# Thirty-two recurrent rounds of an RWKV-7 and attention kernel: loop written out, group norm's end one round later, front steps in another order

## The reference

```python
def rwkv7_layer(h, ...):                       # layer A
    proj = token_shift(rmsnorm(h, norm) @ w_in, mu)   # u + mu * (prev - u)
    r, k, v, z = ...                           # 1024 columns each
    w_lo, a_lo = ...                           # 64 columns each
    w_log = -softplus(-(decay_bias + tanh(w_lo) @ decay_up)) - 0.5
    decay = exp(-exp(w_log))
    a = sigmoid(iclr_bias + a_lo @ iclr_up)
    kk = k * k_k, divided by its norm over each head
    k = k * (1 + (a - 1) * k_a)
    # per head and token:
    #   sa = S @ (-kk_t)
    #   S  = S * w_t + sa (kk_t * a_t)^T + v_t k_t^T
    #   y_t = S @ r_t
    y = group_norm(y) * gn_w + gn_b            # per head
    bonus = sum(r * k * r_k) * v               # per head
    return h + ((y + bonus) * silu(z)) @ w_out
# then one shared k, v and forget gate, and layer B: causal softmax attention
# with the gate's bias, * silu(z), output projection, residual
```

## Time and profile before

| | |
|---|---|
| median of 3 runs | 2269.6 us (2264.41 to 2269.76) |
| the profiled execution | 2273.93 us, its span 2272.2 us |
| TensorE busy | 2010.6 us, 88% of the span |
| VectorE, ScalarE, GpSimd busy | 1049.2, 1011.8 and 238.2 us |

### The profile page before, as it was taken

One profiled execution on the slowest core, in us unless ns is written; L12 is line 12 of the kernel. 1 busy time (PEld: TensorE's weight loads), 2 busy tenths in 40 slices (PEclk: granted clock), 3 DMA queues, 4 the chain that ended last, 5 costly groups with the idle time before them and its releaser, 6 DMA issues.

```text
span 2272.2 us, 59485 instructions
## 1 busy us (share of the span) xinstructions
PE 2010.6 (88%) x24895; PEld 1710.4 (75%) x24895; DVE 1049.2 (46%) x1967; ACT 1011.8 (45%) x1735; POOL 238.2 (10%) x253
## 2 busy tenths in 40 slices
PE   6699989989898998999879789999899999989799
PEld 4687878878787887888769577777777777777477
DVE  2546556556556655665632443333333333333411
ACT  3444444444434444343431243555656464555621
POOL 0011111111111111111100021010101101010000
PEclk9899999999999999999969898999999999999799
DMA  5101000010100001010122211010001000010233
GB/s 189 47 2 44 5 26 26 10 39 7 42 7 26 24 7 44 7 42 7 54 84 85 94 31 29 19 37 19 28 28 28 28 19 29 18 37 9 75 111 111
DMA packets 103569, 89.44 MB, mean 39 GB/s; under 512 B 3973, under 2 KB 95736, under 8 KB 103112
## 3 DMA queue, kind: packets, MB, share of 16 engines
q1 hardware_dynamic: 100120, 68.50, 10.3%
q0 software_dynamic: 3040, 17.14, 2.0%
q10 hardware_dynamic: 208, 0.66, 0.1%
HBM read 64.96 MB, written 21.33 MB: 38 GB/s over the span
## 4 chain that ended last, share of the span: by engine, by line
PE 71%; DVE 11%; ACT 8%; issue 7%; DMA 2%; ACTq 0%; SPq 0%; DVEq 0%; POOLq 0%
PE ps L1661 6%; PE ps L1972 6%; PE ps L1973 6%; PE ps L1974 6%; PE ps L2049 5%; PE ps L1765 5%; PE ps L1662 4%; PE ps L1663 4%; PE ps L1597 2%; PE ps L1599 2%; PE ps L1598 2%; PE ps L1794 2%; PE ps L2007 2%; PE ps L1789 2%; PE ps L2033 2%
## 5 line engine op out<-in xcount | busy, mean ns | idle before, releaser
L1661 PE MATMUL ps<-xh,wh 128*128 128x258 f32 (+1 forms) x1024 | 323.7, 316 | 43.9 <-DVE arena L1275 22.9
L1662 PE MATMUL ps<-xh,wl 128*128 128x258 f32 (+1 forms) x1024 | 290.9, 284 | 0.0
L1663 PE MATMUL ps<-xl,wh 128*128 128x258 f32 (+1 forms) x1024 | 290.7, 284 | 0.0
L1972 PE MATMUL ps<-xh,wh 128*128 128x348 f32 x768 | 260.6, 339 | 19.7 <-ACT arena_b L1094 14.5
L1661 PEld LDWEIGHTS ps<-xh,wh 128*128 128x128 f32 x1024 | 193.2, 189 | 83.4 <-DVE arena L1275 28.4
L1973 PE MATMUL ps<-xh,wl 128*128 128x348 f32 x768 | 255.1, 332 | 0.0
L1974 PE MATMUL ps<-xl,wh 128*128 128x348 f32 x768 | 254.2, 331 | 0.0
L1546 DVE TENSOR_REDUCE arena_b<-ps 128x1 f32<-128x144 f32 (+4 forms) x224 | 106.8, 506 | 273.1 <-PE ps L2011 157.8
L2049 PE MATMUL ps<-arena_b 128*128 128x512 f32 (+4 forms) x448 | 186.7, 501 | 9.8 <-ACT arena_b L1118 9.8
L1662 PEld LDWEIGHTS ps<-xh,wl 128*128 128x128 f32 x1024 | 193.9, 189 | 0.9
L1663 PEld LDWEIGHTS ps<-xl,wh 128*128 128x128 f32 x1024 | 193.5, 189 | 0.0
(11 more groups left out here) (252 smaller groups left out, 4384.4 us busy)
## 6 DMA issues: line engine op xcount, KB each, us to landing
wr<-in_w_in SPq DMA_DIRECT2D x33, 512.0 KB, 4.3
xt_scr<-arena POOLq DMA_DIRECT2D x2, 4176.0 KB, 13.3
wr<-in_kv_w SPq DMA_DIRECT2D x16, 512.0 KB, 4.0
wr<-in_b_w_in SPq DMA_DIRECT2D x16, 512.0 KB, 4.1
arena<-xt_scr SPq DMA_DIRECT2D x8, 522.0 KB, 4.7
arena<-oa_scr SPq DMA_DIRECT2D x8, 520.0 KB, 3.6
arena<-in_x SPq DMA_DIRECT2D x8, 512.0 KB, 3.5
wr<-in_w_out SPq DMA_DIRECT2D x8, 512.0 KB, 4.6
```

Source lines behind the costliest of these rows:

```text
L1661: pe.matmul(bank, wh[:, j, k, :], xh[:, k, t], start=(k == 0), stop=False)
L1662: pe.matmul(bank, wl[:, j, k, :], xh[:, k, t], start=False, stop=False)
L1663: mm = pe.matmul(bank, wh[:, j, k, :], xl[:, k, t], start=False, stop=(k == KO - 1))
L1972: pe.matmul(bank[:, 0:SEG], wh[:, slot, k, :], xh[:, k, t], start=(k == 0), stop=False)
```

## The change

- `low` stands by itself in slot 0, behind `amat` and ahead of `chain` and `tr`; what VectorE and GpSimd make of it is now a step `decay`, which stays where `low` was.
- `("r", 2)` goes from slot 5 to slot 4, behind `kks`; what VectorE makes of r beyond the shift is a step `rmul`, behind `("z", 0)`. In slot 5 the order is `gn2`, `("z", 0)`, `rsqrt`, `rmul`.
- `gn3` goes from slot 6 of its round to slot 2 of the next, and a round (8, 2) is added for the last one. `start_pair`, which copies two parameters for `gn3`, goes from s_ = 1 to s_ = 2.
- In s_ = 2 the splits go from slots 4, 5, 6, 7 to 2, 3, 4, 6.
- `Fori` becomes a Python `for` on TensorE, VectorE, ScalarE and GpSimd, so that all rounds are written out.

```diff
-        FRONT_IN = [[("low",), ("k", 0)],
+        FRONT_IN = [[("decay",), ("k", 0)],
                     [("k", 1), ("exps",), ("k", 2)],
                     [("v", 0), ("kraw",), ("v", 1)],
                     [("v", 2), ("r", 0), ("tables",)],
-                    [("r", 1), ("kks",)],
-                    [("r", 2), ("z", 0)],
+                    [("r", 1), ("kks",), ("r", 2)],
+                    [("z", 0), ("rmul",)],
                     [("z", 1), ("anorm",)],
                     [("z", 2), ("bsum",), ("zgate",)]]
...
                     steps += [("amat", (1, 2))]
+                if front and i == 0:
+                    steps += [("low",)]
                 if chain:
                     steps += CHAIN[i]
                 if early and i == 0:
                     steps += [("tr", (1, 2))]
...
-                    fill = fill[:1] + gn2 + fill[1:]
+                    fill = gn2[:1] + fill[:1] + gn2[1:] + fill[1:] if chain else fill[:1] + gn2 + fill[1:]
                 steps += fill
-                if chain and i == 6:
+                if store and i == 2:
                     steps += [("gn3",)]
...
-                    steps += {4: [("split", 0, 0)], 5: [("split", 0, 1)], 6: [("split", 1, 0)],
-                              7: [("split", 1, 1), ("upf",)]}.get(i, [])
+                    steps += {2: [("split", 0, 0)], 3: [("split", 0, 1)], 4: [("split", 1, 0)],
+                              6: [("split", 1, 1)], 7: [("upf",)]}.get(i, [])
...
-            with pool.Fori(0, KO - 2) as p:
+            for p in range(KO - 2):
...
+            round_pool(KO, 2, round_order(2, False, False, False, False, False))
...
                     elif kind == "r":
+                        shift(rr[:, 0:n], 2, Q_NR)
+                    elif kind == "rmul":
                         dve.wait_ge(S.exp_in, F + 1)
...
-                        shift(rr[:, 0:n], 2, Q_NR)
                         dve.wait_ge(S.shifted, 4 * F + 4)
                         dve.tensor_tensor(ar[:, 1, cols], rr[:, 0:n], e_in[:, 0:n], ALU.mult).then_inc(S.r_tilde, 1)
...
-                        if s_ == 1:
+                        if s_ == 2:
                             start_pair()
```

More of the change, by code:

```diff
@@ L499, in build @@
                     [("v", 2), ("r", 0), ("tables",)],
-                    [("r", 1), ("kks",)],
-                    [("r", 2), ("z", 0)],
+                    [("r", 1), ("kks",), ("r", 2)],
+                    [("z", 0), ("rmul",)],
                     [("z", 1), ("anorm",)],
                     [("z", 2), ("bsum",), ("zgate",)]]
-        FRONT_ONLY = sum(FRONT_IN[:5], []) + [("r", 2), ("rsqrt",)] + sum(FRONT_IN[6:], [("z", 0)])
+        FRONT_ONLY = [("low",)] + sum(FRONT_IN[:6], []) + [("rsqrt",)] + sum(FRONT_IN[6:], [])
         EARLY = [[], [("p", 0)], [("x", 0), ("q",)], [("p", 1)], [("x", 1)], [("p", 2)], [("x", 2)], []]
@@ L507, in build, with round_order @@
         CHAIN = [[("chain", 1)], [("chain", 2)], [("chain", 3)], [("y",)], [], [], [], []]
-        def round_order(s_, early, late, chain, front, weights):
+        def round_order(s_, early, late, chain, front, weights, store=True):
             steps = [("amat", (0,)), ("tr", (0,))] if early and s_ == 0 else []
@@ L665, in round_pool @@
                         continue
-                    if kind == "low":
+                    if kind == "decay":
                         pool.wait_ge(S.cumlog, F + 1)
@@ L685, in round_pool @@
                     elif kind == "gn3":
-                        pair, sg = unit_back(p, s_, 2)
+                        pair, sg = unit_back(p, s_, 3)
                         g0, g1 = SEG_T[sg]
-                        if not (isinstance(n2, int) and n2 == 0):
-                            pool.wait_ge(S.out_stored, 16 * n2)
+                        if n3:
+                            pool.wait_ge(S.out_stored, 16 * n3)
                             pool.sem_inc(S.out_free, 1)
[L692 to L695, removed]
+                        pool.wait_ge(S.out_ready, n3 + 1 + NSEG)
+                        pool.dma_start(oa_scr[pair][:, g0:g1], y_t[:, g0:g1]).then_inc(S.out_stored, 16)
             pool.wait_ge(S.xt_stored, 16)
@@ L974, in _ @@
             round_act_a(0, -1, FRONT_ONLY)
[L975 to L978, removed]
+            round_act_a(0, 0, round_order(0, True, False, False, True, False, False))
+            round_act_a(0, 1, round_order(1, True, True, False, True, False, False))
+            round_act_a(0, 2, round_order(2, True, True, True, True, True, False))
+            for p in range(KO - 2):
                 round_act_a(p, 3, round_order(3, True, True, True, True, True))
@@ L990, in _ @@
             round_act_a(KO, 1, round_order(1, False, False, True, False, False))
+            round_act_a(KO, 2, round_order(2, False, False, False, False, False))
             split_row(1, KO - 1)
@@ L1292, in round_dve_a @@
                             src = param(0, NQ * KO).rearrange("p (q k) -> p q k", k=KO)
-                            src = src[:, :, q_:q_ + 1] if isinstance(q_, int) else src[:, :, bass.ds(q_, 1)]
-                            dve.tensor_copy(pp[:, :].unsqueeze(2), src).then_inc(S.pair_params, 1)
+                            if q_:
+                                dve.wait_ge(S.gn_params, q_)
+                            dve.tensor_copy(pp[:, :].unsqueeze(2), src[:, :, q_:q_ + 1]).then_inc(S.pair_params, 1)
+                    elif kind == "decay":
                         dve.wait_ge(S.dec_tanh, F + 1)
@@ L1438, in _ @@
             round_dve_a(0, -1, FRONT_ONLY)
[L1439 to L1442, removed]
+            round_dve_a(0, 0, round_order(0, True, False, False, True, False, False))
+            round_dve_a(0, 1, round_order(1, True, True, False, True, False, False))
+            round_dve_a(0, 2, round_order(2, True, True, True, True, True, False))
+            for p in range(KO - 2):
                 round_dve_a(p, 3, round_order(3, True, True, True, True, True))
@@ L1459, in _ @@
             round_dve_a(KO, 1, round_order(1, False, False, True, False, False))
+            round_dve_a(KO, 2, round_order(2, False, False, False, False, False))
             split_row(1, KO - 1)
@@ L1915, in _ @@
             round_pe_a(0, -1, FRONT_ONLY)
[L1916 to L1919, removed]
+            round_pe_a(0, 0, round_order(0, True, False, False, True, False, False))
+            round_pe_a(0, 1, round_order(1, True, True, False, True, False, False))
+            round_pe_a(0, 2, round_order(2, True, True, True, True, True, False))
+            for p in range(KO - 2):
                 round_pe_a(p, 3, round_order(3, True, True, True, True, True))
@@ L1928, in _ @@
             round_pe_a(KO, 1, round_order(1, False, False, True, False, False))
+            round_pe_a(KO, 2, round_order(2, False, False, False, False, False))
             pe.wait_ge(S.w_lo, N_AO + 3)
```

18 lines of the change are left out of this document (9 added, 9 removed).

## The result

| | before | after |
|---|---|---|
| median of four runs each, us | 2267.8 (2264.4 to 2269.8) | 2185.1 (2184.3 to 2187.2) |
| profiled execution, its span | 2273.9, 2272.2 | 2185.3, 2183.6 |
| TensorE busy | 2010.6 us, 88% | 1980.7 us, 91% |

What follows compares the result with a forecast made beforehand. TensorE, busy 88% of the span, was taken as the bound, so savings count where it stands still or runs slower. 25.2 + 27.9 + 14.6 + 12.9 - 4.9 - 8.4 - 0.6 = 66.7 us, from 2269.6 to 2203; range 2187 to 2228.

Steps and rivals of the forecast that it cites:

- the loop: Recurrent rounds: writing them out removes five jumps back, each costing TensorE 5.1 us; 25.2 us less.
- r's move: r's last part in slot 4: z's wait for the shift is covered in 31 rounds, 0.90 us each; 27.9 us less.
- (a): Slot 3 of rounds (p, 2): the second split delays the centring that `kks` needs; 7 x 0.7, 4.9 us more.
- low: Slot 0, ahead of chain and tr: k's wait for the tanh goes, 31 x 0.56 less 2.8; 14.6 us less.
- gn3: Moved from slot 6 to slot 2 of the next round: the chain's waits for L1391 shrink; 12.9 us less.
- (b): Slot 5 of (p, 2) and (p, 3): `wu` waits 0.6 us behind shift and split on VectorE; 8.4 us more.
- (c): Tail: `gn3` stands between chain and y in two short rounds, mostly under products; 0.6 us more.
- The 2.8 us set aside for (p, 3): Seven rounds (p, 3) with weights: the tanh also needs late-copied pair parameters, so 0.4 us of k's wait stays each.
- Rival 3: The pause comes from the code, not the jump: 2228 us if as often, 2361 if every round; chance 0.03 each.
- The 1.3 of round (7, 3): Part of the chain's saving: three `gn3` instructions, 3 x 0.42, off that round's 2.9 us wait.
- Rival 2: Waits return on VectorE's queue, with `wu` held up in every round: 2227 us, range 2214 to 2236; chance 0.22.
- Rival 4: More gain: the added waits at `kks` and `wu` don't appear; 2190 us, range 2183 to 2193; chance 0.14.

Runs made afterwards that it cites:

- the last kernel: The changed kernel with the splits of (p, 2) and (p, 3) moved to other places, none in slot 4; 2167.2 us, 0.9547 of the kernel before.

## Why the prediction fell short

The direction was right, and the mechanisms and sizes of the loop, of r's move and of (a) were nearly so. Two terms were too small, `low` by 13.3 us and `gn3` by up to 7.4, and a cost that had no term, the new pauses, took 3.9 back. The forecast time, 2203, is 17.9 us above the measured one: 15.9 from the sum, and 1.8 because the kernel before has a median of 2267.8 and not 2269.6.

| term | forecast | measured | by |
|---|---|---|---|
| loop | 25.2 | 24.7 | written out alone |
| r in slot 4, with (b) | 27.9 - 8.4 = 19.5 | 19.4 | r put back |
| `low` ahead | 14.6 | 27.9 | `low` put back (26.2 alone) |
| `gn3` | 12.9 | 20.3 | `gn3` alone |
| (a) `kks` | -4.9 | -6.1 | 7 x 0.87, start to start |
| new issue waits | 0 | -3.9 | 0.95 + 1.11 + 1.82, last section |
| sum | 66.7 (with (c), -0.6) | 82.3 | the change: 82.6 |

That the terms add up to within 0.3 us of the change is luck. Each is the difference of two medians that are known to some 4 us. The pauses are counted twice, too: 2.1 us are in the term of r and 1.3 in that of `gn3` already, and `gn3` is 16.8 instead of 20.3 by what lies in the rounds. What stands is the order of the errors, with that of `low` the largest. (c), 0.6 us, has no measurement of its own.

**`low`, the step that failed.** The prediction said: "I take the idle time here, since I have no row of what would follow `low` unawaited". It had priced r's wait from start to start, 0.90 us where the bracket had 0.66, and did not do so here. The two stretches, TensorE in slot 0 of round (6, 2), first before, then after; start, length, instruction, idle time:

```profile
959.85 1.10 PE L1723 MATMUL ps<-arena 64*64 64x128 f32 x32
961.15 0.33 PE L1882 MATMUL ps<-arena 64*64 64x64 f32 x4 [0.20 <-DVE arena L1410]
961.41 1.09 PE L1737 MATMUL ps<-ident,arena 128*128 128x128 f32 x8
962.44 0.48 PE L1672 MATMUL ps<-arena 64*128 64x256 f32 x1
...
963.70 0.39 PE L1661 MATMUL ps<-xh,wh 128*128 128x258 f32 x1 [0.56 <-ACT arena L870]
```

```profile
884.36 1.10 PE L1728 MATMUL ps<-arena 64*64 64x128 f32 x32
885.39 0.48 PE L1677 MATMUL ps<-arena 64*128 64x256 f32 x1
...
886.02 0.33 PE L1887 MATMUL ps<-arena 64*64 64x64 f32 x4
886.28 1.09 PE L1742 MATMUL ps<-ident,arena 128*128 128x128 f32 x8
887.13 0.36 PE L1666 MATMUL ps<-xh,wh 128*128 128x258 f32 x1
```

From `amat` to k it is 963.70 - 959.85 = 3.85 us, and 887.13 - 884.36 = 2.77 after: 1.08 less. Three parts make it up here. `low` to what follows it was 1.26 and is 0.63 (the tanh's wait, 0.63 and not 0.56). `amat` to what follows it was 1.30 and is 1.03: `low` now fills the time in which the chain's second step had waited for VectorE. And the transposes to what follows them, 1.03 and 0.85. Neither of the last two was in the sum: the earlier trace rows begins at the transposes, one row behind the chain's wait. The chain's wait is one of those that the prediction passed over as not as long as its four. The 2.8 us set aside for (p, 3) were right, though: k still waits for the tanh there, in all seven rounds and in the first round of all (8 times, 3.5 us), and putting `low` back cost 0.60 us in these rounds against 1.01 and 1.08 in (p, 1) and (p, 2), 0.4 less as predicted. So what was too small is the 0.56 of a round: by the put-back it is 27.9 / 31 = 0.90 us on average, with the rounds (p, 3) counted in, where the forecast had 14.6 / 31 = 0.47. `low` alone, 26.2, says the same from the other side.

ScalarE shows that the tanh did what was said. In the same slot of after it starts 0.78 us after `low`, ahead of the row copies, and is through 0.1 us before k:

```profile
886.17 0.47 ACT L871 ACTIVATE arena<-ps,pp 128x256 f32<-128x256 f32 x1 [1.47 <-PE ps L1677]
886.54 0.47 ACT L876 ACTIVATE arena<-ps,pp 128x256 f32<-128x256 f32 x1
886.98 1.09 ACT L931 ACTIVATE arena<-ps 128x512 f32<-128x512 f32 x2
```

**The loop.** Right, in size and in cause. Rival 3 is out as the cause of the old pauses: written out alone has none of their size. But the prediction also said that it is wrong if issue waits turn up between the rounds, and that sign did show. There are three, of 1.0 to 1.8 us, two of them in the rounds, and the forecast had put them at nothing.

**r in slot 4.** The cover is there: z starts 0.35 us after `gn2` (0.34 in round (6, 0): 845.91, 846.25), as the prediction read from the earlier trace rows, and the term is 31 x 0.93 (1.01 from `kks` to z, less 0.08 from z to `wu`).

**(b)** was right in size, 7 x 0.65 and 7 x 0.63, and half wrong in place. In (p, 2) it is `wu`, as forecast: VectorE of after in round (6, 2), with the shift, the split, the mask and the adds in the order of the earlier trace rows with the split between:

```profile
904.53 0.48 DVE L1277 SCALAR_TENSOR_TENSOR arena<-ps,pp,arena 128x256 f32<-128x256 f32 x1 [0.79 <-ACT arena L842]
905.04 0.69 DVE L1243 TENSOR_TENSOR wl<-wr,wh 128x512 fp32r<-128x512 f32 x1
905.65 0.42 DVE L1370 TENSOR_TENSOR arena<-ps,levels 128x256 f32<-128x256 f32 x1
906.10 0.86 DVE L1387 TENSOR_TENSOR arena<-ps,arena 64x256 f32<-64x256 f32 x2
```

and TensorE, which waits for the last of them, done at 906.96:

```profile
907.11 0.66 PE L1829 MATMUL ps<-arena 64*64 64x128 f32 x8 [0.48 <-DVE arena L1387]
```

In (p, 3) the split is that of z's own weights, and z is the next product. TensorE waits for it there, and comes to `wu` late enough:

```profile
936.01 0.36 PE L1666 MATMUL ps<-xh,wh 128*128 128x272 f32 x1 [0.38 <-DVE wl L1243]
```

The prediction asked of a split only whom it holds up on VectorE, not who reads what it makes.

**gn3, the other term that was too small.** The places were right: 12.5 us at the chain in (p, 0) and (p, 2) where 11.6 were forecast, and 1.2 in (p, 3), which the sum did not have. The 1.3 of round (7, 3) hardly came: its wait of 2.9 us is 2.7 with `gn3` alone. That VectorE would run ahead in slot 0 as well was not counted. In the full change these 4 us and those of `low` may overlap in part; the sum of the table doesn't show it. `gn3` did fit in slot 2: VectorE of after, round (6, 1), its three instructions without a wait and 1.67 us of idle time behind them:

```profile
863.46 0.42 DVE L1431 TENSOR_TENSOR arena<-arena 128x256 f32<-128x256 f32 x1
863.91 0.49 DVE L1433 SCALAR_TENSOR_TENSOR arena<-arena,gp 128x256 f32<-128x256 f32 x1
864.44 0.48 DVE L1436 SCALAR_TENSOR_TENSOR arena<-arena,gp 128x256 f32<-128x256 f32 x1
866.59 0.43 DVE L1370 TENSOR_TENSOR arena<-ps,levels 128x256 f32<-128x256 f32 x1 [1.67 <-PE ps L1770]
```

The first takes 0.42 us here, where L1427 took 0.95. GpSimd's first product of this slot starts at 864.99, behind all three, so the overlap that the prediction allowed for did not come about here.

**(a)** The mechanism was right. VectorE of after in round (6, 2) waits for ScalarE's half, and the centring is behind it:

```profile
900.49 0.69 DVE L1243 TENSOR_TENSOR wl<-wr,wh 128x512 fp32r<-128x512 f32 x1 [1.39 <-ACT wh L803]
901.10 0.42 DVE L1370 TENSOR_TENSOR arena<-ps,levels 128x256 f32<-128x256 f32 x1
901.43 0.68 DVE L1383 TENSOR_TENSOR arena<-ps,arena 128x512 f32<-128x512 f32 x1
902.03 0.43 DVE L1425 SCALAR_TENSOR_TENSOR arena<-ps,arena 128x272 f32<-128x272 f32 x1
```

```profile
902.61 0.67 PE L1700 MATMUL ps<-arena,head_ones 128*128 128x256 f32 x2 [0.70 <-DVE arena L1425]
```

The bracket is the 0.7 of the forecast; from start to start it is 0.87, the same kind of error as for `low`, 1.2 us in all.

Rival 2 is out: `wu` waits in seven rounds and not in all. Rival 4 gave 2190, nearest to the time, for a reason that did not hold: (a) and (b) both appeared. The 2185 us lie within that rival's own span, 2183 to 2193, of which the range given took in only the part from 2187.

## What to carry to other kernels

Price a wait from start to start, over the whole stretch from the last instruction that is not touched to the next one, and not by the idle time in brackets: here the brackets had 0.56 and the move was worth 0.9 us a round. A step that is moved ahead also fills whatever wait stood at its new place, so read that place's rows too. Of a step that is put between others ask both whom it holds up on its engine and who reads its result next. A better place for the small steps, worth 17.9 us here, could be read from the list of waits after the first change.

## What the hardware showed that I had not expected

Written-out code pauses too, though rarely. TensorE of after, in the middle of `mm` of (5, 3):

```profile
818.30 0.28 PE L1868 MATMUL ps<-arena 64*64 64x64 f32 x4
819.70 0.27 PE L1868 MATMUL ps<-arena 64*64 64x64 f32 x2 [1.11 <-issue]
```

There are two more, 0.95 us at 576.87 and 1.82 at 1081.10, the latter behind the last `kks`. Around the one shown, in the DMA view of 812 to 822 us, a load of 512 KB of weights and the packets that carry instructions pass through the same engines:

```profile
q1 hardware_dynamic: 1040, 0.52, 18.0%
q8 instruction: 2, 0.03, 1.4%
q14 instruction: 1, 0.01, 0.2%
```

The trace has the same load around the pause at 576.87, but none around the longest one, at 1081.10. What all three share is a packet of 16 KB on the queue of the instructions that lands 1.2 to 1.4 us before TensorE goes on (575.51, 818.50, 1079.86); in the first two it starts as the load ends. Such packets come every 1 to 12 us, so one near a pause is weak evidence. So that TensorE waited for its instructions is argued from three places, that the load had held them up from two, and no run was made to test either. The pauses differ from kernel to kernel. Written out alone has none in the rounds and 0.6 us behind the last `kks`; every kernel with `gn3` moved has one of 1.8 to 2.4 us there; and the two in the rounds are absent with r back, with `gn3` alone and in the last kernel.
